# Attention products with the values stationary, and the router's transposes ahead of its logits

## The chip, the cores and the metric

The kernel runs on one core of a Trainium2 chip. The metric is the device time of one execution in microseconds. The kernel before took 1974.58 us, the median of three runs (1971.63 to 1975.39). TensorE (PE) is granted one of two clocks, 1.2 or 2.4 GHz; the profile prints the granted clock of a stretch as a share of the higher one.

## The reference

A decoder trunk of two layers over 256 tokens of 1024 channels in float32. Each layer has a token mixer and a feed-forward part, dense in layer 0 and routed to 2 of 8 experts in layer 1.

```
def _masked_softmax(s, mask):
    s = jnp.where(mask, s, NEG_INF)
    return jnp.where(mask, jax.nn.softmax(s, axis=-1), 0.0)
def token_mixing(h, ...):
    (nq, ..., mg) = split(h @ w_in)
    o_nsa = sum over (cmp, sel, win) of g_branch * softmax(q k) @ v   # 8 heads in 2 groups
    o_ret = silu(g) * normalised(retention(q, k, v))
    o_fox = softmax(q k * scale + decay) @ v                          # 8 heads, each with its own v
    merged = gates0*(o_nsa @ w_read_nsa) + gates1*(o_ret @ w_read_ret) + gates2*(o_fox @ w_read_fox)
    return merged @ w_out
def moe_ffn(h, ...):
    top_v, top_i = top_k(h @ w_router, 2)
    return sum over experts of gate * swiglu(h, w1[e], w3[e], w2[e])
```

## The kernel before

Weights come in chunks of 1 MB. ScalarE (ACT) copies a half of a chunk to `w_hi`, VectorE (DVE) makes the rest `w_lo`, and PE multiplies three pairs for each product (`mm3`, L746 to L748). The splits run `AHEAD` = 3 halves in front of PE.

In the token mixer the attention is spread over the projection. The string `SLOTS` (L189) is an order by hand: each slot names steps of the attention, then a quarter of a projection block (12 `mm3` steps, some 2.8 us of PE). The calls are `CALLS`, nine of them: 0 cmp, 1 sel, 2 win (head group 0), 3 cmp, 4 sel, 5 win (group 1), 6 retention, 7 and 8 fox. In a slot, `a1:5` turns the queries of call 5, `a2` and `a3` are its scores on PE and their mask and row maximum on DVE, `e0` and `e1` the exponentials on ACT for the first and the second 128 tokens, `b1` and `b2` PE's transposes of these probabilities from `S` by way of PSUM (`pT`) into `PT`, `b3` the product with the values (for cmp it goes with `b2`), `o` the transposes of a finished mixer's output and `s`, `d` pieces of the adaLN columns. Every engine walks the same string; DVE ends a slot with the piece's copies (`ended`) and the next split (`split_to`).

The product with the values (`attention_values`, L966 to L997) holds 128 x 128 probabilities stationary and moves 64 columns of values, so the result has tokens on partitions. DVE's `values` (L2134) then takes the reciprocal of the row sums, multiplies by the branch's gate, scales the result out of PSUM and adds it up in `o_sb`. At `o` PE turns `o_sb` in eight transposes, and ACT and DVE split the turned rows.

The router of layer 1 stands between the mixer and the experts: the normalised rows `y` are turned (`rows_T`), DVE scales them into `hf`, PE multiplies them with the router's weights `routw` (`logits`), a piece of the adaLN product follows (`ada_pair`, tiles `raw,csilu`), then the counts of the chosen (`rs,tab`), the gather of rows per expert (`sel,y`), and the experts' products.

Of the kernel before, what the change touches and what calls it, by code (L numbers as in the profile page):

```python
# [31 lines left out]
P = 128  # L32
# [312 lines left out]
P_COUNT = {"cmp": 1, "sel": 2, "win": 2, "ret": 0, "fox": 2}  # L345
S_SIGNALS = sum(S_COUNT[k] for k, _ in CALLS)
# [3 lines left out]
def build(nc, a, table, out):  # L350
    ctx = ExitStack()
    with ctx:
# [179 lines left out]
        p_ready = sem("p_ready")  # L532
        var_ready = sem("var_ready")
# [191 lines left out]
        def _(pe):  # L725
# [222 lines left out]
            def probabilities(sub, c, l):  # L948
# [4 lines left out]
                if kind == "cmp":  # L953
                    pe.wait_ge(p_ready, p_at + 1)
                    for t in range(TT):
                        turned([s[:, (t * HG + h) * 16:(t * HG + h) * 16 + NCMP] for h in range(HG)], P)
                elif sub == "b1":
                    pe.wait_ge(p_ready, p_at + 1)
                    turned([s[:, h * P:(h + 1) * P] for h in range(HG)], P)
                else:  # L960
                    pe.wait_ge(p_ready, p_at + 2)
# [4 lines left out]
            def attention_values(sub, c, l):  # L966
# [13 lines left out]
                dst = take_O()  # L980
                if kind == "cmp":
                    for t in range(TT):
                        for h in range(HG):
                            at = t * HG * HD + h * HD
                            ins = mm(dst[:, at:at + HD], PT[0:NCMP, (t * HG + h) * P:(t * HG + h + 1) * P], vc[0:NCMP, g, :])
                    ins.then_inc(O_full, 1)
                    return
                v0 = {"sel": C_NVS + g * HD, "win": C_NVW + g * HD, "fox": C_FV + g * HG * HD}[kind]
                vs = HD if kind == "fox" else 0
                for h in range(HG):  # L990
                    mm(dst[:, h * HD:(h + 1) * HD], PT[:, h * P:(h + 1) * P], proj[:, 0, v0 + h * vs:v0 + h * vs + HD])
                for h in range(HG):
                    for m in range(2):
                        at = (HG + h * 2 + m) * P
                        ins = mm(dst[:, (HG + h) * HD:(HG + h + 1) * HD], PT[:, at:at + P],
                                 proj[:, m, v0 + h * vs:v0 + h * vs + HD], m == 0, m == 1)
# [82 lines left out]
            for l in range(DEPTH):  # L1079
# [12 lines left out]
                for subs, kind, which, i in MIXES[l]:  # L1092
                    for sub, c in subs:
# [19 lines left out]
                        elif sub == "o":  # L1113
# [117 lines left out]
                else:  # L1231

                    dst = take_A()
# [8 lines left out]

                    logits(0)
                    rows_T(2, 3)
                    logits(1)
                    rows_T(3, 4)
# [11 lines left out]
                    ada_sum_early()  # L1258
                    pe.wait_ge(slots_ready, 1)
# [163 lines left out]
        def _(act):  # L1423
# [208 lines left out]
            for l in range(DEPTH):  # L1632
# [32 lines left out]
                for subs, kind, which, i in MIXES[l]:  # L1665
# [3 lines left out]
                    for sub, c in subs:  # L1669
# [17 lines left out]
                        elif sub in ("b1", "b2") and (t_uses(sub, c) or CALLS[c][0] == "ret"):  # L1687
                            evacuate_p(sub, c)
                        elif sub == "o":
# [141 lines left out]
        def _(dve):  # L1831
# [302 lines left out]
            def values(sub, c, l):  # L2134
# [24 lines left out]
                p_at = P_SIGNALS * l + sum(P_COUNT[k] for k, _ in CALLS[:c])  # L2159
                if kind == "cmp":  # L2160
                    if c == 0:
                        dve.wait_ge(sig_ready, 2 * l + 1)
                    dve.wait_ge(p_ready, p_at + 1)
                    sv = s[:, 0:P].rearrange("p (r n) -> p r n", n=16)[:, :, 0:NCMP]
                    link(V.tensor_reduce(st[:, 16:24], sv, AX_X, ALU.add))
                else:
                    dve.wait_ge(p_ready, p_at + 2)
                link(V.reciprocal(st[:, 24:32], st[:, 16:24]))
                coef = st[:, 24:32]
                if kind != "fox":  # L2170
                    coef = st[:, 32:40]
                    branch = {"cmp": 0, "sel": 1, "win": 2}[kind]
                    cv = coef.rearrange("p (t h) -> p t h", t=TT)
                    link(V.tensor_tensor(cv, st[:, 24:32].rearrange("p (t h) -> p t h", t=TT),
                                         gates3[:, :, branch * 8 + g * HG:branch * 8 + (g + 1) * HG], ALU.mult))
                    if kind == "cmp":
                        link(V.tensor_tensor(cv, cv, bc(cvalid.unsqueeze(2), [P, TT, HG]), ALU.mult))
                po, free = O_in()
                width = HG * HD
                src = po[:, :].rearrange("p (t h d) -> p t h d", t=TT, h=HG)  # L2180
                dst = o_sb[:, :, g * width:(g + 1) * width].rearrange("p t (h d) -> p t h d", h=HG)
                cf = coef.rearrange("p (t h) -> p t h", t=TT)
# [429 lines left out]
```

## Time and profile before

| what | value |
|---|---|
| median of three runs | 1974.58 us |
| the profiled execution | 1973.35 us, span 1971.6 us |
| mean granted clock | 0.985 |
| PE, DVE, ACT busy | 96%, 74%, 58% of the span |
| token mixers | about 50 to 355 us and 592 to 905 us |
| dense part | about 355 to 584 us |
| router, experts | 905 to 952 us, 952 to 1950 us |

In a timeline row the first number is the start in microseconds from the start of the span, the second the length, then engine, line, operation, output tile, input tiles, shapes and the number of instructions in the group; a bracket holds the idle time ahead of it and what ended it. A float32 product of the program shows as two instructions, a transpose as one. In a row of windows stand the window, its length, the busy time of each engine with its number of instructions, the granted clock, the share of the DMA engines and GB/s. In a row of grouped lines the last fields are busy us, mean ns of one, and idle before.

### The profile page before, as it was taken

The page shows a single profiled execution, that of the slowest core. Times are in us where ns is not written, and L with a number is a line of the kernel's source. Part 1 is how long each engine was busy: PE and PEld are TensorE (multiplying, and loading weights), DVE is VectorE, ACT ScalarE, POOL GpSimd, SP SyncE. Part 2 cuts the span into 40 slices and gives each one's busy share as a digit, 9 for nine tenths or more (in the row PEclk, how much of TensorE's full clock was granted, in tenths as well). Part 3 has the DMA queues.
Part 4 walks back from the last instruction along what each step waited for, and adds up shares of the span by engine and source line. Part 5 has one row for each costly group of instructions (what it writes and reads, how often), then busy time and mean ns, then how long its engine had stood idle before and what let it go on. Part 6 is the DMA issues. An engine that isn't in the chain of part 4 may idle for free.

```text
span 1971.6 us, 29864 instructions
## 1 busy us (share of the span) xinstructions
PE 1897.5 (96%) x10960; PEld 1472.4 (75%) x10960; DVE 1459.5 (74%) x1507; ACT 1141.8 (58%) x1245; POOL 92.4 (5%) x134
## 2 busy tenths in 40 slices
PE   5999999999999999998999999999999999999996
PEld 3878888789987888887776676766766767667774
DVE  3755565745567655657788888889888888888988
ACT  1544554334435545542567767777677676767773
POOL 0510100000004201000000000000000000000000
PEclk9999999999999999998899999999999999999998
DMA  8846435595557644353799999999999999999993
GB/s 316 290 155 233 152 128 171 198 332 183 185 192 232 221 150 150 128 171 129 278 371 343 354 343 358 353 343 355 343 362 354 342 346 349 355 348 345 358 365 135
DMA packets 275638, 533.10 MB, mean 270 GB/s; under 512 B 10768, under 2 KB 23392, under 8 KB 275424
## 3 DMA queue, kind: packets, MB, share of 16 engines
q1 hardware_dynamic: 275552, 531.91, 76.5%
q8 instruction: 60, 0.98, 0.2%
q14 instruction: 26, 0.21, 0.0%
HBM read 530.83 MB, written 1.05 MB: 270 GB/s over the span
## 4 chain that ended last, share of the span: by engine, by line
PE 86%; DVE 7%; ACT 3%; DVEq 2%; issue 1%; DMA 1%; SPq 0%; ACTq 0%
PE pA L746 17%; PE pA L747 17%; PE pA L748 17%; PE pA L751 8%; PE pO L751 7%; PE pO L746 5%; PE pO L747 5%; PE pO L748 5%; PE pT L804 3%; DVE w_lo L1851 1%; DVEq L2486 1%; DVE wide_lo L1896 1%; ACT w_hi L1434 1%; ACT wide_hi L1434 1%; DMA raw<-in_ffn_w 1%
## 5 line engine op out<-in xcount | busy, mean ns | idle before, releaser
L1896 DVE TENSOR_TENSOR wide_lo<-raw,wide_hi 128x2048 fp32r<-128x2048 f32 x336 | 761.6, 2290 | 120.6 <-ACT wide_hi L1434 101.6
L1434 ACT ACTIVATE wide_hi<-raw 128x2048 fp32r<-128x2048 f32 x336 | 644.3, 1920 | 212.0 <-PE pO L748 118.1
L1434 ACT ACTIVATE w_hi<-raw 128x1024 fp32r<-128x1024 f32 (+1 forms) x242 | 251.2, 1045 | 334.8 <-PE pA L748 235.8
L1851 DVE TENSOR_TENSOR w_lo<-raw,w_hi 128x1024 fp32r<-128x1024 f32 (+1 forms) x242 | 294.3, 1230 | 167.0 <-ACT w_hi L1434 157.9
L746 PE MATMUL pA<-wide_hi,x_lo 128*96 128x512 f32 x896 | 356.4, 398 | 1.6 <-DVE wide_lo L1896 1.0
L747 PE MATMUL pA<-wide_lo,x_hi 128*96 128x512 f32 x896 | 353.7, 395 | 0.0
L748 PE MATMUL pA<-wide_hi,x_hi 128*96 128x512 f32 x896 | 351.0, 392 | 0.0
L746 PE MATMUL pA<-w_hi,h_lo 128*128 128x512 f32 (+2 forms) x560 | 226.1, 404 | 14.7 <-DVE w_lo L1851 10.8
L748 PE MATMUL pA<-w_hi,h_hi 128*128 128x512 f32 (+2 forms) x560 | 216.8, 387 | 0.0
L747 PE MATMUL pA<-w_lo,h_hi 128*128 128x512 f32 (+2 forms) x560 | 216.7, 387 | 0.0
L746 PEld LDWEIGHTS pA<-wide_hi,x_lo 128*96 128x96 f32 x896 | 144.6, 161 | 65.3 <-issue 3.5
L748 PEld LDWEIGHTS pA<-wide_hi,x_hi 128*96 128x96 f32 x896 | 144.7, 162 | 63.0
L747 PEld LDWEIGHTS pA<-wide_lo,x_hi 128*96 128x96 f32 x896 | 144.4, 161 | 57.0
L746 PE MATMUL pO<-wide_hi,aT_lo 128*96 128x512 f32 x448 | 178.8, 399 | 1.1 <-DVE aT_lo L2454 1.1
L747 PE MATMUL pO<-wide_lo,aT_hi 128*96 128x512 f32 x448 | 176.5, 394 | 0.0
L748 PE MATMUL pO<-wide_hi,aT_hi 128*96 128x512 f32 x448 | 175.7, 392 | 0.0
L746 PEld LDWEIGHTS pA<-w_hi,h_lo 128*128 128x128 f32 x560 | 106.7, 191 | 41.9 <-issue 17.5
L748 PEld LDWEIGHTS pA<-w_hi,h_hi 128*128 128x128 f32 x560 | 106.7, 191 | 22.9
L747 PEld LDWEIGHTS pA<-w_lo,h_hi 128*128 128x128 f32 x560 | 107.1, 191 | 19.1
L751 PE MATMUL pA<-h_hi,w_lo 128*128 128x256 f32 x352 | 99.0, 281 | 0.8 <-DVE w_lo L1851 0.6
L751 PE MATMUL pA<-h_hi,w_hi 128*128 128x256 f32 x352 | 98.3, 279 | 0.0
L751 PE MATMUL pA<-h_lo,w_hi 128*128 128x256 f32 x352 | 98.3, 279 | 0.0
(273 smaller groups left out, 2272.7 us busy)
## 6 DMA issues: line engine op xcount, KB each, us to landing
raw<-in_moe_w SPq DMA_DIRECT2D x336, 1024.0 KB, 7.2
raw<-in_w_in SPq DMA_DIRECT2D x56, 1024.0 KB, 6.4
raw<-in_ada_w SPq DMA_DIRECT2D x48, 1024.0 KB, 6.8
raw<-in_ffn_w SPq DMA_DIRECT2D x33, 1024.0 KB, 5.2
raw<-in_w_out SPq DMA_DIRECT2D x8, 1024.0 KB, 5.1
raw<-in_cmp_k_w SPq DMA_DIRECT2D x4, 1024.0 KB, 7.7
raw<-in_cmp_v_w SPq DMA_DIRECT2D x4, 1024.0 KB, 11.1
raw<-in_w_read_nsa SPq DMA_DIRECT2D x4, 1024.0 KB, 6.1
```

The source lines that it names most:

```text
L746: nc.tensor.matmul(dst, xl, wh, start=first, stop=False, skip_group_check=True)
L747: nc.tensor.matmul(dst, xh, wl, start=False, stop=False, skip_group_check=True)
L748: return nc.tensor.matmul(dst, xh, wh, start=False, stop=last, skip_group_check=True)
L751: return nc.tensor.matmul(dst, lhsT, rhs, start=first, stop=last, skip_group_check=True)
L804: ins = nc.tensor.transpose(pt[0:m, i * width:i * width + n], src, ident[0:n, 0:n])
L1434: return nc.scalar.activation(dst, src, ACT.Copy)
L1851: V.tensor_tensor(w_lo[m][:, 0:n], raw[s][:, i * n:(i + 1) * n], w_hi[m][:, 0:n].bitcast(F32), ALU.subtract).then_inc(raw_done, 1)
L1896: V.tensor_tensor(wide_lo[m][:, :], raw[g][:, :], wide_hi[m][:, :].bitcast(F32), ALU.subtract).then_inc(raw_done, 2)
L2486: dve.drain().then_inc(gather_free, 1)
```

## The change

Values become stationary: in `attention_values` PE loads 64 columns of values and moves the turned probabilities, the even heads to output partitions 0 to 63 and the odd ones to 64 to 127. The result comes out turned, so at `o` of calls 0 and 2 (the sparse attention and fox) PE transposes nothing; ACT and DVE split `o_sb` directly. Scaling by the reciprocal sum and the gate can no longer follow the product, since tokens are then on the free axis: the new `scaled(t, c, l)` on DVE multiplies the probabilities in `S` in place, half by half, and signals `p_scaled`, for which PE's `b1` and `b2` now wait instead of `p_ready`. DVE's `values` is left with one copy or one addition. The list `LATE` holds calls 4 and 5, whose `b1` and `e1` share a slot. At the router `rows_T` of the next quarter precedes `logits`, and `keep_clock` multiplies zeros 8 times before the logits and 10 times after `ada_sum_early`.

```diff
@@ -343,6 +343,7 @@
+LATE = [c for subs, *_ in SLOTS for sub, c in subs if sub == "b1" and ("e1", c) in subs]
@@ -951,14 +953,14 @@
                 if kind == "cmp":
-                    pe.wait_ge(p_ready, p_at + 1)
+                    pe.wait_ge(p_scaled, p_at + 1)
                     for t in range(TT):
...
                 elif sub == "b1":
-                    pe.wait_ge(p_ready, p_at + 1)
+                    pe.wait_ge(p_scaled, p_at + 1)
                     turned([s[:, h * P:(h + 1) * P] for h in range(HG)], P)
                 else:
-                    pe.wait_ge(p_ready, p_at + 2)
+                    pe.wait_ge(p_scaled, p_at + 2)
                     for p0 in range(0, HG, 2):
@@ -978,22 +980,30 @@
+                rows_of = lambda odd: dst[odd * HD:(odd + 1) * HD, :]
...
-                    for t in range(TT):
-                        for h in range(HG):
-                            at = t * HG * HD + h * HD
-                            ins = mm(dst[:, at:at + HD], PT[0:NCMP, (t * HG + h) * P:(t * HG + h + 1) * P], vc[0:NCMP, g, :])
+                    late = PT[0:NCMP, 0:2 * HG * P].rearrange("p (t j o n) -> p t j o n", t=TT, j=2, o=2)
+                    for odd in range(2):
+                        ins = mm(rows_of(odd).rearrange("p (t j n) -> p t j n", t=TT, j=2), vc[0:NCMP, g, :], late[:, :, :, odd, :])
...
-                vs = HD if kind == "fox" else 0
-                for h in range(HG):
-                    mm(dst[:, h * HD:(h + 1) * HD], PT[:, h * P:(h + 1) * P], proj[:, 0, v0 + h * vs:v0 + h * vs + HD])
-                for h in range(HG):
-                    for m in range(2):
-                        at = (HG + h * 2 + m) * P
-                        ins = mm(dst[:, (HG + h) * HD:(HG + h + 1) * HD], PT[:, at:at + P],
-                                 proj[:, m, v0 + h * vs:v0 + h * vs + HD], m == 0, m == 1)
+                first = PT[:, 0:HG * P].rearrange("p (j o n) -> p j o n", j=2, o=2)
+                second = PT[:, HG * P:3 * HG * P].rearrange("p (j o m n) -> p j o m n", j=2, o=2, m=2)
+                steps = [(0, 0, True, True), (1, 0, True, False), (1, 1, False, True)]
+                if kind == "fox":
+                    for j in range(2):
+                        for t, m, opens, closes in steps:
+                            for odd in range(2):
+                                c0 = v0 + (2 * j + odd) * HD
+                                p_t = first[:, j, odd, :] if t == 0 else second[:, j, odd, m, :]
+                                ins = mm(rows_of(odd)[:, (2 * t + j) * P:(2 * t + j + 1) * P], proj[:, m, c0:c0 + HD], p_t, opens, closes)
+                else:
+                    for t, m, opens, closes in steps:
+                        for odd in range(2):
+                            p_t = first[:, :, odd, :] if t == 0 else second[:, :, odd, m, :]
+                            ins = mm(rows_of(odd)[:, t * SEQ:(t + 1) * SEQ].rearrange("p (j n) -> p j n", j=2),
+                                     proj[:, m, v0:v0 + HD], p_t, opens, closes)
@@ -1110,7 +1120,7 @@
-                        elif sub == "o":
+                        elif (sub, c) == ("o", 1):
@@ -1230,6 +1240,16 @@
+                    spare = pA[b.A.slot(b.A.n + 3)]
+                    evacuated(b.A, A_free, 4)
+                    def keep_clock(n):
+                        for _ in range(n):
+                            mm(spare[:, :].rearrange("p (k n) -> p k n", k=CK), zeros[:, :],
+                               zeros[:, :].unsqueeze(1).broadcast_to([P, CK, P]))
+                    keep_clock(8)
@@ -1240,10 +1260,10 @@
+                    rows_T(2, 3)
...
-                    rows_T(2, 3)
+                    rows_T(3, 4)
...
-                    rows_T(3, 4)
@@ -1256,6 +1276,7 @@
                     ada_sum_early()
+                    keep_clock(10)
                     pe.wait_ge(slots_ready, 1)
@@ -1686,6 +1707,11 @@
+                        elif sub == "o" and c != 1:
+                            act.wait_ge(o_ready, 3 * l + c + 1)
+                            for q in range(2):
+                                copy(oT_hi[c][:, 2 * q:2 * q + 2, :].rearrange("p j (t n) -> p t j n", t=TT),
+                                     o_sb[:, q, :].rearrange("p (t j n) -> p t j n", t=TT, j=2)).then_inc(oT_hi_ready, 1)
@@ -2156,40 +2182,40 @@
                     return
-                p_at = P_SIGNALS * l + sum(P_COUNT[k] for k, _ in CALLS[:c])
+                po, free = O_in()
+                dst = o_sb[:, g, :]
+                if kind in ("cmp", "fox"):
+                    V.tensor_copy(dst, po[:, :]).then_inc(free, 1)
+                else:
+                    V.tensor_tensor(dst, dst, po[:, :], ALU.add).then_inc(free, 1)
+                freed(b.O, O_free)
+                if c in WHOLE:
+                    dve.drain().then_inc(o_ready, 1)
+            def scaled(t, c, l):
+                kind, g = CALLS[c]
+                st = stat[:, (c % 2) * 40:(c % 2) * 40 + 40]
+                s = S[c % 2]
+                dve.wait_ge(p_ready, P_SIGNALS * l + sum(P_COUNT[k] for k, _ in CALLS[:c]) + t + 1)
                 if kind == "cmp":
...
                         dve.wait_ge(sig_ready, 2 * l + 1)
-                    dve.wait_ge(p_ready, p_at + 1)
                     sv = s[:, 0:P].rearrange("p (r n) -> p r n", n=16)[:, :, 0:NCMP]
                     link(V.tensor_reduce(st[:, 16:24], sv, AX_X, ALU.add))
+                    t0, nt, width = 0, TT, NCMP
                 else:
-                    dve.wait_ge(p_ready, p_at + 2)
-                link(V.reciprocal(st[:, 24:32], st[:, 16:24]))
-                coef = st[:, 24:32]
+                    t0, nt, width = t, 1, (t + 1) * P
+                    sv = s[:, HG * P * t:HG * P * t + HG * width].rearrange("p (h n) -> p h n", h=HG)
+                at = slice(24 + t0 * HG, 24 + (t0 + nt) * HG)
+                link(V.reciprocal(st[:, at], st[:, 16 + t0 * HG:16 + (t0 + nt) * HG]))
                 if kind != "fox":
-                    coef = st[:, 32:40]
                     branch = {"cmp": 0, "sel": 1, "win": 2}[kind]
-                    cv = coef.rearrange("p (t h) -> p t h", t=TT)
-                    link(V.tensor_tensor(cv, st[:, 24:32].rearrange("p (t h) -> p t h", t=TT),
-                                         gates3[:, :, branch * 8 + g * HG:branch * 8 + (g + 1) * HG], ALU.mult))
+                    cv = st[:, at].rearrange("p (t h) -> p t h", t=nt)
+                    link(V.tensor_tensor(cv, cv, gates3[:, t0:t0 + nt, branch * 8 + g * HG:branch * 8 + (g + 1) * HG], ALU.mult))
                     if kind == "cmp":
                         link(V.tensor_tensor(cv, cv, bc(cvalid.unsqueeze(2), [P, TT, HG]), ALU.mult))
-                po, free = O_in()
-                width = HG * HD
-                src = po[:, :].rearrange("p (t h d) -> p t h d", t=TT, h=HG)
-                dst = o_sb[:, :, g * width:(g + 1) * width].rearrange("p t (h d) -> p t h d", h=HG)
-                cf = coef.rearrange("p (t h) -> p t h", t=TT)
-                for t in range(TT):
-                    to = dst[:, t] if kind in ("cmp", "fox") else o_part[:, t * width:(t + 1) * width].rearrange("p (h d) -> p h d", h=HG)
-                    ins = V.tensor_tensor(to, src[:, t], bc(cf[:, t].unsqueeze(2), [P, HG, HD]), ALU.mult)
-                ins.then_inc(free, 1)
-                freed(b.O, O_free)
-                if kind in ("sel", "win"):
-                    both = o_sb[:, :, g * width:(g + 1) * width]
-                    link(V.tensor_tensor(both, both, o_part[:, :].rearrange("p (t n) -> p t n", t=TT), ALU.add))
-                if c in WHOLE:
-                    dve.drain().then_inc(o_ready, 1)
+                V.tensor_tensor(sv, sv, bc(st[:, at].unsqueeze(2), [P, nt * HG, width]), ALU.mult).then_inc(p_scaled, 1)
@@ -2246,6 +2272,9 @@
+                        if sub == "b2" and c in LATE:
+                            scaled(1, c, l)
+                    for sub, c in subs:
@@ -2256,6 +2285,12 @@
+                        elif sub == "o" and c != 1:
+                            for q in range(2):
+                                dve.wait_ge(oT_hi_ready, 6 * l + 2 * c + q + 1)
+                                turns = lambda to: to[c][:, 2 * q:2 * q + 2, :].rearrange("p j (t n) -> p t j n", t=TT)
+                                V.tensor_tensor(turns(oT_lo), o_sb[:, q, :].rearrange("p (t j n) -> p t j n", t=TT, j=2),
+                                                turns(oT_hi).bitcast(F32), ALU.subtract).then_inc(oT_ready, 1)
@@ -2270,6 +2305,11 @@
+                    for sub, c in subs:
+                        if sub == "e0" and CALLS[c][0] == "cmp" or sub == "e1":
+                            scaled(0, c, l)
+                        elif sub == "b1" and CALLS[c][0] in ("sel", "win", "fox") and ("e1", c) not in subs:
+                            scaled(1, c, l)
```

DVE around call 5 (`win`, group 1), from the mask of its last scores (`S_108<-pO,tab`) over the projection's copies to the next splits, before:

```order
L2059 TENSOR_TENSOR S_108<-pO,tab 128x512 [waits O_full]
L2065 TENSOR_REDUCE stat<-S_108 128x4 [waits O_free0]
L2066 TENSOR_SCALAR stat<-stat 128x4 [waits dve_link]
L2168 RECIPROCAL stat<-stat 128x8 [waits p_ready]
L2174 TENSOR_TENSOR stat<-stat,gates_80 128x8 [waits dve_link]
L2185 TENSOR_TENSOR tmp<-pO,stat 128x256 [waits O_full,dve_link]
L2185 TENSOR_TENSOR tmp<-pO,stat 128x256
L2190 TENSOR_TENSOR o_sb<-o_sb,tmp 128x2x256 [waits O_free1]
L1866 TENSOR_TENSOR mod<-pT,cols 128x4 [waits T_full,dve_link]
L2201 COPY proj<-pA 128x512 [waits half_used] x2
L1851 TENSOR_TENSOR w_lo_62<-raw_54,w_hi_58 128x1024 [waits hi_ready]
```

and the same place on DVE now:

```order
L2085 TENSOR_TENSOR S_108<-pO,tab 128x512 [waits O_full]
L2091 TENSOR_REDUCE stat<-S_108 128x4 [waits O_free0]
L2092 TENSOR_SCALAR stat<-stat 128x4 [waits dve_link]
L2190 TENSOR_TENSOR o_sb<-o_sb,pO 128x512 [waits O_full]
L1892 TENSOR_TENSOR mod<-pT,cols 128x4 [waits T_full,O_free1]
L2227 COPY proj<-pA 128x512 [waits half_used] x2
L1877 TENSOR_TENSOR w_lo_62<-raw_54,w_hi_58 128x1024 [waits hi_ready]
L2211 RECIPROCAL stat<-stat 128x4 [waits p_ready]
L2215 TENSOR_TENSOR stat<-stat,gates_80 128x4 [waits dve_link]
L2218 TENSOR_TENSOR S_108<-S_108,stat 128x512 [waits dve_link]
```

The values' five instructions of call 4 shrank to one addition, and behind the copies and a split stands the scaling of call 5's first half, which `b1:5` on PE waits for.

PE at the router, from the adaLN sum (`tab,acc`) over the turned rows (`tab,y`) to the logits (`routw,hf`), before:

```order
L870 MATMUL pO<-tab,acc 128x128 [waits O_free1,O_free0]
L751 MATMUL pA<-routw,hf 128x8 [waits hf_ready,A_free2]
L751 MATMUL pA<-routw,hf 128x8 x3
L804 MATMUL pT<-tab,y 128x128 [waits T_free0,y_ready]
L804 MATMUL pT<-tab,y 128x128 x3
L751 MATMUL pA<-routw,hf 128x8 [waits hf_ready]
L751 MATMUL pA<-routw,hf 128x8 x3
L804 MATMUL pT<-tab,y 128x128 [waits T_free1]
L804 MATMUL pT<-tab,y 128x128 x3
```

and PE at the router now:

```order
L872 MATMUL pO<-tab,acc 128x128 [waits O_free1,O_free0]
L753 MATMUL pA<-zeros 128x512 [waits A_free0,A_free1,A_free3,A_free2]
L753 MATMUL pA<-zeros 128x512 x7
L806 MATMUL pT<-tab,y 128x128 [waits T_free0,y_ready,A_free2]
L806 MATMUL pT<-tab,y 128x128 x3
L753 MATMUL pA<-routw,hf 128x8 [waits hf_ready]
L753 MATMUL pA<-routw,hf 128x8 x3
L806 MATMUL pT<-tab,y 128x128 [waits T_free1]
L806 MATMUL pT<-tab,y 128x128 x3
```

Eight products of zeros stand ahead, and each group of transposes moved one group of logits forward.

## Rows read from the trace of the kernel before

**Rows 1.** Windows: us, busy of PE, PEld, DVE, ACT, POOL, clock, DMA, GB/s

```profile
137.00:205.00 68.00, 68.00 (x601) 56.11 (x600) 37.42 (x64) 31.53 (x80) 1.87 (x1) 1.00 0.57 201
...
952.00:1950.00 998.00, 995.57 (x4560) 704.06 (x4559) 874.00 (x633) 708.63 (x547) 0.00 (x0) 1.00 0.96 345
```

**Rows 2.** Timeline of PE, call 1's value product and its neighbours

```profile
137.68 1.13 PE L751 MATMUL pO<-kT,qT 64*128 64x256 f32 x4
...
142.47 2.79 PE L751 MATMUL pO<-proj,PT 128*128 128x64 f32 x24
145.19 0.64 PE L751 MATMUL pO<-raw,csilu 128*32 128x128 f32 x16
```

**Rows 3.** Timeline of PE, call 3's value product to call 4's first transposes

```profile
177.41 1.99 PE L751 MATMUL pO<-vc,PT 15*128 15x64 f32 x16
179.33 0.50 PE L746 MATMUL pA<-w_hi,h_lo 128*128 128x512 f32 x1
...
182.44 0.60 PE L804 MATMUL pT<-tab,S 128*128 128x128 f32 x4
```

**Rows 4.** Timeline of PE, the output's transposes of the sparse attention

```profile
228.37 1.04 PE L804 MATMUL pT<-tab,o_sb 128*128 128x128 f32 x8
229.16 0.48 PE L746 MATMUL pA<-w_hi,h_lo 128*128 128x512 f32 x1
```

**Rows 5.** Timeline of PE, router

```profile
918.35 1.95 PE L751 MATMUL pO<-raw,csilu 128*32 128x128 f32 x64
...
925.09 1.71 PE L751 MATMUL pA<-routw,hf 128*128 128x8 f32 x8 [2.21 <-DVE hf L1999]
...
936.91 2.30 PE L751 MATMUL pA<-rs,tab 128*128 128x8 f32 x10
...
942.57 6.93 PE L751 MATMUL pA<-sel,y 128*128 128x96 f32 x32 [3.05 <-DVE mod L1866]
...
951.61 0.47 PE L746 MATMUL pA<-wide_hi,x_lo 128*96 128x512 f32 x1 [0.29 <-DVE x_lo L2439]
```

**Rows 6.** Lines of DVE by shape, 100 to 300 us

```profile
L1851 DVE TENSOR_TENSOR w_lo<-raw,w_hi 128x1024 fp32r<-128x1024 f32 x41 | 51.0, 1249 | 17.9 <-ACT w_hi L1434 15.5
...
L2185 DVE TENSOR_TENSOR tmp<-pO,stat 128x256 f32<-128x256 f32 x8 | 3.0, 419 | 12.9 <-PE pO L751 12.9
L2190 DVE TENSOR_TENSOR o_sb<-o_sb,tmp 128x512 f32<-128x512 f32 x4 | 2.8, 693 | 0.1
...
L2168 DVE RECIPROCAL stat<-stat 128x8 f32<-128x8 f32 x8 | 1.6, 197 | 0.1
```

**Rows 7.** Timeline of DVE around calls 4 and 5

```profile
181.31 1.23 DVE L1851 TENSOR_TENSOR w_lo<-raw,w_hi 128x1024 fp32r<-128x1024 f32 x1
...
195.51 1.22 DVE L2065 TENSOR_REDUCE stat<-S 128x4 f32<-128x1024 f32 x1
...
199.27 1.28 DVE L2201 COPY proj<-pA 128x512 f32<-128x512 f32 x2
```

**Rows 8.** Timeline of PE, call 5's first transposes

```profile
200.31 0.60 PE L804 MATMUL pT<-tab,S 128*128 128x128 f32 x4
```

**Rows 9.** Windows around idle stretches and at the router, columns as in rows 1

```profile
110.00:112.00 2.00, 0.48 (x4) 0.37 (x4) 0.00 (x0) 1.99 (x4) 0.00 (x0) 1.00 0.96 371
113.00:119.00 6.00, 6.00 (x15) 4.26 (x14) 3.27 (x6) 1.13 (x2) 0.00 (x0) 0.50 0.01 3
661.00:669.00 8.00, 6.48 (x35) 5.08 (x34) 3.71 (x8) 5.31 (x7) 0.00 (x0) 1.00 0.26 100
926.00:949.00 23.00, 19.95 (x141) 19.03 (x142) 12.39 (x39) 2.30 (x4) 0.00 (x0) 0.50 0.48 173
```

**Rows 10.** Timeline of DVE, router

```profile
925.16 0.99 DVE L1999 TENSOR_SCALAR hf<-pT,mod 128x256 f32<-128x256 f32 x2
...
931.44 2.29 DVE L1896 TENSOR_TENSOR wide_lo<-raw,wide_hi 128x2048 fp32r<-128x2048 f32 x1 [0.21 <-issue]
```

**Rows 11.** Timeline of PE, products of zeros within the experts

```profile
974.37 0.61 PE L751 MATMUL pO<-zeros 128*128 128x512 bf16 x2
```

More of the change, by code:

```diff
@@ L532, in build @@
         p_ready = sem("p_ready")
+        p_scaled = sem("p_scaled")
         var_ready = sem("var_ready")
```

## The prediction

> **What bounds the kernel now.** I read the windows by stage first: the reader is to see which engine is full in each. In the token mixer's middle PE is busy for all of 68 us and DVE for 37.42, at granted clock 1.00; in the experts PE is busy 995.57 of 998 us [rows 1]. So in both PE's own work sets the time, and DVE costs only where PE is made to wait for it. The experts follow the router with no slack, so what the router gains reaches the end in full. Then the timelines of PE for the price of each changed piece, those of DVE for what a new wait would meet, and the windows around idle stretches for the clock. In the router PE runs at 0.50 from 926 to 949 us [rows 9]: every product there costs double.
>
> The sum is made against the profiled execution, 1973.35 us; the median of the runs shown is 1.2 us above it.
>
> **Values stationary (removes PE time).** A product with the values of sel, win and fox is 24 instructions and takes 145.19 - 142.47 = 2.72 us, 0.113 each [rows 2]. Now it is 12 instructions for sel and win with 256 columns moved, or 24 for fox with 128 columns, and two of them, for the even and the odd heads, write different halves of the output partitions. The trace has no pair of 64-column products. The nearest row is the adaLN piece with 32 columns: 64 float32 instructions of 128 columns in 1.95 us [rows 5], so 0.12 us for every four, where the value product shows 0.113 us for one of only 64 columns: the four run side by side. I take two abreast for 64 columns, at 0.12 us a pair of 128 columns: fox 12 x 0.12 = 1.46, sel and win 6 x 0.24 = 1.46. For cmp, 1.92 us before [rows 3], there are 4 instructions of 512 columns, 2 x 0.49 = 0.98. Changing between full and split columns costs a little; in rows 2 the adaLN piece starts 0.07 us before the modelled end of the value product, so I take 0.1 a call. A call of sel, win or fox gains 2.72 - 1.56 = 1.16 us, a cmp 1.92 - 1.08 = 0.84 us. With 12 and 4 such calls in two layers: 13.9 + 3.4 = 17.3 us. The other end: nothing side by side. A group of four 256-column float32 instructions takes 1.13 us, 0.28 each [rows 2], which makes 12 x 0.28 = 3.4 us and a loss of 0.7 a call.
>
> The Trainium skill, "TensorEngine Tiling (Array Packing)", Theoretical Speedup, gives up to 2x for 64 columns; the row of four abreast agrees. The same page speaks against the change in Key Properties: changing the tiling mode drains the engine. If a drain cost a whole 256-column instruction of 0.28 us at the entry and at the exit (an estimate from rows 2), 16 calls would pay 9 us instead of my 1.6 and the forecast would be 1970; the early start of the adaLN piece in rows 2 speaks against that.
>
> **No transposes at `o`.** Eight transposes take 229.16 - 228.37 = 0.79 us [rows 4]; two such steps in each layer go: 3.2 us. ACT and DVE do there what they did, from another source. PE gains 17.3 + 3.2 = 20.5 us.
>
> **Scaling ahead of the transposes (adds DVE time and waits).** DVE's prices: 1.25 us for 1024 columns, 0.69 for 512, 0.42 for 256, 0.20 for a small one [rows 6]. A call of sel or win loses two small ones, two of 256 and one of 512 (1.93) and gains four small ones, 512 and 1024 scaled and one of 512 added (3.4): +1.5 us; fox +2.0, cmp about +0.1. A layer: 4 x 1.5 + 2 x 2.0 + 0.2 = 10 us. On the average that lies in DVE's idle 30 of 68 us [rows 1]. But `b1` and `b2` on PE now wait for it, and all of PE's later products queue behind them. At two places there is no slack, since `b1` and `e1` share a slot and the scaling stands behind a split.
>
> Call 4: the split that ended at 181.31 + 1.23 = 182.54 [rows 7] comes 1.0 earlier, as the four small ones and two of 256 of call 3 make way for one of 512 (1.64 - 0.69); the scaling of 512 with two small ones is 1.1, so it is done at 182.7. PE arrives at 182.44 - 0.84 = 181.6 [rows 3]. Wait 1.1 us.
>
> Call 5: DVE's row maximum ends at 195.51 + 1.22 = 196.73; then one small one, the addition of 0.69, one small one, the copies of 1.28 [rows 7], a split of 1.25 and the scaling of 1.1: 201.5. PE arrives at 200.31 - 1.16 = 199.15 [rows 8]. Wait 2.4 us.
>
> For the other scaled halves I find slack of 0.3 to 0.7 us in the slots, and allow 1 us a layer, an estimate. Waits: 4.5 a layer, 9 us in all; between 4 (half of it, if the slots behind take some up) and 20 (all of DVE's added time).
>
> **The clock in the mixers.** At 110.1 us PE idles 1.5 us, and from 113 to 119 us the clock is 0.50; the same wait near 661 us leaves it at 1.00 [rows 9]. Six us at half clock do three us of work: 3 us lost. I charge the two waits at call 5 with 2.5 us each, 5 in all; ends 0 and 12 (four waits at 3).
>
> **The router.** At full clock, the transposes moved ahead let DVE make its four pairs of `hf` one behind the other from 925.16 on at 0.99 each [rows 10]: done at 928.2, the split of 2.29 at 930.5 instead of 933.7, 3.2 earlier. The counts would halve (2.30 to 1.15) and the gather too (6.93 to 3.47) [rows 5]: 3.2 + 1.15 + 3.47 = 7.8, or some 8 with the end of the piece that delays the counts now. The zeros: 0.61 us for two with the tail of the second [rows 11], some 0.23 each, so 8 take 1.8 us in an idle time of 2.21 and 10 take 2.3 in one of 3.05 [rows 5]: nothing at full clock; without that cover 4.1 us. But a new gap opens: PE ends the adaLN piece near 930.6 (1.95 at full clock) and the counts wait for DVE until 933.4, 2.8 us without zeros. By the idle of 1.5 us above I expect half clock after it, over counts and zeros: counts from 933.4 to 935.7, a short piece of adaLN and zeros of 4.5 us to 940.7, and the gather at full clock again to 944.1, where it ended at 942.57 + 6.93 = 949.5 [rows 5]: 5.4 us. I take 5.5; ends 8 and a loss of 1 (half clock all through, zeros of 4.5 us in the 3.05).
>
> **Sum.** -20.5 + 9 + 5 - 5.5 = -12: 1961.4 us for the profiled execution, 1962.6 for the median. I predict 1963 us.
>
> **Rivals.** (a) The router stays at half clock; the zeros don't help. For it: it fell after the idle of 2.21 us [rows 5], and the zeros leave some 0.4 of that. Against: 1.8 of it is filled. -20.5 + 9 + 5 + 1 = -5.5: 1969. (b) The 64-column products don't run side by side, since the row that I read is of another width. Sel and win lose 0.7 each (8 x 0.7 = 5.6), fox with 24 at 0.12 loses 0.2 (0.8), cmp 4 x 0.5 = 2.0 loses 0.1 (0.4), `o` gains 3.2; PE arrives later, so about 1 us of wait a layer remains (2), with one fall of the clock (2.5). 5.6 + 0.8 + 0.4 - 3.2 + 2 + 2.5 - 5.5 = +2.6: 1977, no change by 0.2%. (c) Slower: DVE becomes the pace-maker of the attention slots. Its splits stand behind the scaling in the same queue, PE waits at each `b1` and `b2`, and each of the four long waits drops the clock: -20.5 + 20 + 12 - 5.5 = +6: 1981. It decides from the point where over 14 of the 20 us that DVE gains come out on PE's path. For it: the scaling is in the path of every call; against it, DVE's idle 45% in rows 1. (d) The waits are half as long, no clock is lost, the router holds: -20.5 + 4.5 - 8 = -24: 1951.
>
> **Chances.** Forecast 0.45 (its own range 1956 to 1967), (a) 0.22, (b) 0.12, (c) 0.09, (d) 0.12. What a measurement of this kernel can tell from no change is about 0.2%, 4 us: 1970.6 to 1978.5. Faster takes the forecast, (d) and most of (a): 0.77; the same takes (b) and the rest of (a): 0.14; slower is (c): 0.09. Leaving out (c) and the outer parts of (b) and (d), the range is 1950 to 1974.
>
> **What would show it.** In the profile after, the value products of sel and win should take 1.4 to 1.6 us between their start and the next group's (3.2 to 3.4 would be rival b); PE should wait for DVE's scaling at `b1` of call 4 (1.1) and call 5 (2.4) in both layers, with a clock of 0.50 behind the second; the gap after the adaLN piece in the router should be 2 to 3 us, and the first expert's product come near 939.6 us instead of 951.61 [rows 5], all of the sum. The prediction is wrong if PE's waits in a mixer exceed 8 us, if the router's clock stays 0.50 up to the experts, or if the experts' stretch changes length at all, since nothing in it changed.

## The result and the profile after

The changed kernel took 1962.9 us, the median of five runs (1960.09 to 1963.92); the ratio to the kernel before is 0.994, with a 95% interval of 0.9928 to 0.9951. The prediction was 1963. The profiled execution took 1960.09 us, its span is 1958.3 us.

The timeline of PE after, at call 1 (which answers to [rows 2]), at the first transposes of calls 4 and 5 ([rows 3, 8]) and in the router ([rows 5]); the columns are those of the rows before:

```profile
140.76 1.51 PE L753 MATMUL pO<-PT,proj 128*64 128x256 f32 x12
142.21 1.95 PE L753 MATMUL pO<-raw,csilu 128*32 128x128 f32 x64
...
178.54 0.66 PE L806 MATMUL pT<-tab,S 128*128 128x128 f32 x4 [0.88 <-DVE S L2218]
...
197.50 0.66 PE L806 MATMUL pT<-tab,S 128*128 128x128 f32 x4 [2.10 <-DVE S L2218]
...
912.65 1.95 PE L753 MATMUL pO<-raw,csilu 128*32 128x128 f32 x64
915.98 1.09 PE L806 MATMUL pT<-tab,y 128*128 128x128 f32 x8 [1.38 <-DVE y L2015]
...
917.02 1.89 PE L753 MATMUL pA<-zeros 128*128 128x512 bf16 x8
...
923.86 3.60 PE L753 MATMUL pO<-raw,csilu 128*32 128x128 f32 x64
927.52 1.28 PE L753 MATMUL pA<-rs,tab 128*128 128x8 f32 x10
...
928.80 2.32 PE L753 MATMUL pA<-zeros 128*128 128x512 bf16 x10
932.12 3.81 PE L753 MATMUL pA<-sel,y 128*128 128x96 f32 x32 [1.00 <-DVE mod L1892]
...
938.03 0.48 PE L748 MATMUL pA<-wide_hi,x_lo 128*96 128x512 f32 x1 [0.29 <-DVE x_lo L2479]
```

The reader is to see: twelve products in 142.21 - 140.76 = 1.45 us where 24 took 2.72; two waits for DVE's scaling (`S`, L2218) that were not there; and a router whose counts and gather run at full speed (1.28 and 3.81 us, where [rows 5] has 2.30 and 6.93) while the adaLN piece ahead of them takes 3.60 where it took 1.95. What PE waits for in the layers, as engine and line waited for, us in total, times and longest, for the mixer of layer 0:

```profile
PE pT L806 <- DVE S L2218: 3.3, 3, 2.1
PE pO L753 <- ACT kT L1455: 1.5, 1, 1.5
```

Only the first line is new; layer 1 shows the same 3.3 us, and 0.9 more at the forget gates (`DVE fox`). The windows of the changed kernel behind the idle time ahead of call 1, behind the wait of call 5 in layer 0 and around it in layer 1, and in the router, columns as in [rows 1]:

```profile
113.00:119.00 6.00, 6.00 (x18) 4.30 (x17) 3.74 (x10) 0.27 (x2) 0.00 (x0) 0.56 0.01 3
199.00:203.00 4.00, 4.00 (x54) 3.18 (x45) 0.00 (x0) 1.92 (x9) 0.00 (x0) 1.00 0.68 213
738.00:740.00 2.00, 0.40 (x2) 0.40 (x3) 1.93 (x5) 0.67 (x1) 0.00 (x0) 0.89 0.00 0
740.00:743.00 3.00, 3.00 (x52) 2.51 (x54) 0.69 (x1) 2.24 (x8) 0.00 (x0) 0.51 0.02 5
924.00:927.00 3.00, 3.00 (x60) 2.77 (x62) 2.78 (x10) 0.22 (x1) 0.00 (x0) 0.50 0.02 5
928.00:937.00 9.00, 8.00 (x62) 6.56 (x62) 6.60 (x25) 1.81 (x2) 0.00 (x0) 1.00 0.88 309
```

PE's group starts, aligned piece by piece with those of before, give the steps in layer 0: a call of sel, win or fox is 1.17 us shorter (1.28 of the product less 0.10 ahead of it for sel), a cmp 0.92, each `o` 0.87; the wait of call 4 takes back 1.04, that of call 5 2.27, `b2:5` 0.45. From the keys of call 1 to the end of the mixer that is 6.1 us less in layer 0. In layer 1 of the two profiled executions the same steps gave nothing on balance: half-clock stretches in the mixer (592 to 905 us) cost PE 4.9 us after and nothing before (busy time weighted with what the clock lacked of 1.00, in windows of 2 us). From the router's adaLN piece to the first expert's product it is 25.4 us after and 33.3 before. The profiles' split into mixers and router thus hangs on where the clock happened to be low, and the runs have to decide it.

One stretch that the change does not touch grew: the dense part, from PE's wait for `h_lo` behind the mixer of layer 0 to its wait of 3.0 us for `y` ahead of layer 1's, took 232.1 us before and 233.4 after. Behind a wait of 2.1 us for DVE's `mod`, which both kernels have, the clock fell in the second profile alone (the kernel before, then the changed one):

```profile
426.00:434.00 8.00, 4.83 (x28) 4.05 (x29) 4.49 (x9) 1.74 (x3) 0.00 (x0) 1.00 1.05 389
420.00:428.00 8.00, 5.53 (x26) 4.88 (x27) 3.54 (x6) 1.53 (x2) 0.00 (x0) 0.79 1.05 393
```

### The profile page after: what moved, and what is told of

Read it like the earlier page. It is cut to its first block, busy times and chain, and to the rows that moved or that the text cites. A ratio compares the mean times of both kernels' runs of the same rounds, so it can differ in the third digit from the quotient of the medians.

```text
span 1958.3 us, 29535 instructions
## 1 busy us (share of the span) xinstructions
PE 1880.5 (96%) x10802; PEld 1438.2 (73%) x10802; DVE 1478.7 (76%) x1531; ACT 1143.9 (58%) x1245; POOL 95.6 (5%) x134
## 4 chain that ended last, share of the span: by engine, by line
PE 83%; DVE 9%; ACT 3%; DMA 2%; DVEq 2%; issue 1%; SPq 1%; ACTq 0%
PE pA L748 17%; PE pA L749 16%; PE pA L750 16%; PE pA L753 8%; PE pO L748 5%; PE pO L749 5%; PE pO L750 5%; PE pO L753 5%; PE pT L806 3%; DVE w_lo L1877 2%; DVE wide_lo L1922 1%; DMA tab<-in_tables 1%; DVEq L2526 1%; ACT w_hi L1455 1%; ACT wide_hi L1455 1%
```

## The experiments

All were timed in five rounds beside the kernel before, whose medians in the three groups were 1974.22, 1974.08 and 1973.56 us.

**The parts alone.** The value products, the `o` and the scaling with the old router:

```
-                    spare = ...; evacuated(b.A, A_free, 4); def keep_clock(n): ...
-                    keep_clock(8)
-                    rows_T(2, 3); logits(0); rows_T(3, 4); logits(1)
+                    logits(0); rows_T(2, 3); logits(1); rows_T(3, 4)
-                    keep_clock(10)
```

> The new value products, the output without transposes and the scaling ahead, with the router as before. My theory, by which the router's stretch lost 33.26 - 25.38 = 7.9 us and the rest of the gain is the mixers': 1962.9 + 7.9 = 1971 us, 4 us below before, with PE waits for DVE's scaling of about 0.9 and 2.1 us at calls 4 and 5. Rival (the whole gain is the router's, the mixers give back in waits and clock what PE saves): 1974 to 1975 us.

Measured: 1966.17 us, ratio 0.9964 (0.9952 to 0.9976). And the reverse, the new router on the kernel before:

```
+                    spare = ...; evacuated(b.A, A_free, 4); def keep_clock(n): ...
+                    keep_clock(8)
-                    logits(0); rows_T(2, 3); logits(1); rows_T(3, 4)
+                    rows_T(2, 3); logits(0); rows_T(3, 4); logits(1)
+                    keep_clock(10)
```

> The kernel before with the router's new order and the zeros alone. My theory: 1974.6 - 7.9 = 1966.7 us, the first expert's product about 8 us earlier. Rival (the router's clock was held only by chance in the profiled execution, the mixers carry the gain): 1970 us or more. Rival (all of the gain is the router's): 1963 us.

Measured: 1969.86 us, ratio 0.9976 (0.9967 to 0.9985). Both of my numbers missed, and in the same sense: by the medians the mixers give 8.0 us (4.7 to 9.5 by the interval) and the router 4.4 (3.0 to 6.5). Together 12.4, the change's own 11.7 within the noise, so as far as the intervals tell the parts add. The 7.9 us read from one pair of profiles was too much for the router: over all the profiles of this section, the stretch from the router's adaLN piece to the first expert's product takes 25.4 to 27.7 us with both groups of zeros (seven profiles) and 31.1 to 33.3 without any (three), and the pair that I compared first lies nearly at the two ends. In the profile of the router alone, half clock lay over the counts and most of the second zeros, and the gather ran at full clock:

```profile
934.03 2.30 PE L751 MATMUL pA<-rs,tab 128*128 128x8 f32 x10
...
936.44 3.61 PE L751 MATMUL pA<-zeros 128*128 128x512 bf16 x10
939.88 3.74 PE L751 MATMUL pA<-sel,y 128*128 128x96 f32 x32
```

The same profiles show where the mixers' gain is steady. From PE's wait for `win_lo` to its wait for `h_lo`, layer 0's mixer takes 268.6 us in all six profiles with the changed mixers as they are, and 274.8 in both with the old ones. Layer 1's takes 262.9 to 267.3 against 267.5. The dense part behind layer 0 takes 233.4 to 234.9 against 232.1, each time with half clock behind its wait of 2 us; why the clock fell there with the changed mixers and not with the old ones isn't shown.

**The overlap.** The even heads' products first, then the odd ones':

```
-                    for t, m, opens, closes in steps:
-                        for odd in range(2):
+                    for odd in range(2):
+                        for t, m, opens, closes in steps:
```

> The changed kernel, with the products of sel, win and fox in another order: all of the even heads' (partitions 0 to 63), then all of the odd heads' (64 to 127), so that two neighbours share their 64 columns and cannot run side by side. The same number of instructions and columns. My theory (two abreast): sel and win go from 1.45 to about 3.0 us, fox from 1.46 to 2.9; 8 x 1.6 + 4 x 1.4 = 18 us, of which 3 are taken from the waits at call 5: 1977 to 1980 us. Rival (the gain comes from fewer weight loads, not from running side by side): 1963 us.

Measured: 1967.82 us, ratio 0.9971 (0.996 to 0.9982): 4.9 us above the changed kernel, neither number. The trace shows why. The order undoes the overlap only in part: the starts of the twelve instructions fall into two rows of six, each mostly 0.216 us apart, one from 142.94 and one from 143.43 on. That the second row is the odd half's is read from this spacing; it began when three of the even half's six had yet to start, and not behind the sixth. So a second experiment took the second half of the columns away:

```
-                rows_of = lambda odd: dst[odd * HD:(odd + 1) * HD, :]
+                rows_of = lambda odd: dst[0:HD, :]
```

> The changed kernel with all products with the values written to output partitions 0 to 63, the odd heads over the even ones (it leaves the odd heads' result out), so that no two can run side by side, in whatever order they are taken. My theory (in the kernel with one half first the second half's products still started after two of the first's, so that experiment undid the overlap only in part): 12 products at 0.216 each are 2.6 us for sel and win, 24 at 0.109 are 2.6 for fox, 4 at 0.43 are 1.8 for cmp, so every call loses 1.1 us or 0.8: 12 x 1.1 + 4 x 0.8 = 16 us, less some 4 of the waits for DVE: 1974 to 1976 us, what the kernel before takes; without the overlap the values stationary gain nothing. Rival (the overlap is worth only the 5 us of that experiment): 1968 us.

The whole time, 3004.79 us, says nothing: with the odd heads' results missing the router chooses other rows, as it seems, and the experts take 2050 us instead of 1020. Its mixers can be read. The same product in the timeline of PE with one half first:

```profile
142.94 2.00 PE L753 MATMUL pO<-PT,proj 128*64 128x256 f32 x12
144.87 0.41 PE L753 MATMUL pO<-raw,csilu 128*32 128x128 f32 x5
```

and with all in one half:

```profile
143.78 2.80 PE L753 MATMUL pO<-PT,proj 128*64 128x256 f32 x12
146.52 0.32 PE L753 MATMUL pO<-raw,csilu 128*32 128x128 f32 x4
```

From start to the next group's start: 1.45 us alternating, 1.93 one half first, 2.74 in one half, and 2.72 before (for fox 1.46, 2.38, 2.76 and 2.62). Aligned with the changed kernel, every sel, win and fox call loses 1.29 to 1.30 us and every cmp 0.85. Making the values stationary gains nothing in itself; all of the product's gain is two halves of the columns at work at once. Without it the mixer of layer 0 takes 278.1 us, 3.4 more than before the change, although the transposes at `o` are gone; a fall of the clock near 254 us, which the profile before lacks, is at most 1.7 of that.

**The waits.** DVE scales the first half of calls 4 and 5 one slot earlier, ahead of the copies and the split:

```
-                        if sub == "e0" and CALLS[c][0] == "cmp" or sub == "e1":
+                        if sub == "e0" and (CALLS[c][0] == "cmp" or c in LATE) or sub == "e1" and c not in LATE:
                             scaled(0, c, l)
```

> The changed kernel, with DVE's scaling of the first half for calls 4 and 5 moved one slot forward, behind the first exponentials and ahead of the projection's copies and the split. My theory: the waits of 0.88 and 2.10 us go in both layers, 6 us, and the fall of the clock behind the second of them in layer 1 (1.6 us in the profile) too: 1955 to 1957 us. Rival (DVE sets the pace, the split is late instead and PE waits for weights): 1961 to 1963 us.

Measured: 1954.66 us, ratio 0.9899 (0.9884 to 0.9913), 8.2 us below the changed kernel and just under my numbers. DVE at call 5, from the addition of call 4's values to the split:

```profile
192.73 0.68 DVE L2190 TENSOR_TENSOR o_sb<-o_sb,pO 128x512 f32<-128x512 f32 x1
...
193.92 0.69 DVE L2218 TENSOR_TENSOR S<-S,stat 128x512 f32<-128x512 f32 x1
194.53 1.28 DVE L2227 COPY proj<-pA 128x512 f32<-128x512 f32 x2
195.95 2.36 DVE L1877 TENSOR_TENSOR w_lo<-raw,w_hi 128x1024 fp32r<-128x1024 f32 x2
```

and what PE waits for in the mixer of layer 0:

```profile
PE pO L753 <- ACT kT L1455: 1.5, 1, 1.5
...
PE pA L748 <- DVE w_lo L1877: 0.5, 1, 0.5
PE pT L806 <- DVE S L2218: 0.3, 1, 0.3
```

The waits of 0.88 and 2.10 us are gone, and the split that stood ahead of the scaling costs no more than before (`w_lo` 0.5). DVE had the time; the scaling stood in the wrong place of its queue. 6 of the 8.2 us are these waits. In the two profiles layer 0's mixer is 3.4 us shorter and layer 1's 7.6, with one half-clock stretch of 3.4 us in place of three; that the rest of the 8.2 is the clock is argued, not shown.

**The router's parts.** Without both groups of zeros:

```
-                    keep_clock(8)
-                    keep_clock(10)
```

> The changed kernel without the two groups of zero products; the transposes still stand ahead of the logits. My theory (order and zeros share the router's gain of some 4 us: the order lets DVE's scaled rows follow each other, the zeros keep the clock up for counts and gather): the router at 0.50 for most of its length, the gather 6 to 7 us instead of 3.8: 1965 to 1966 us. Rival (the order alone does it): 1963 us.

Measured: 1967.97 us, ratio 0.9964 (0.9952 to 0.9976), above both numbers. With the zeros and the old order:

```
-                    rows_T(2, 3); logits(0); rows_T(3, 4); logits(1)
+                    logits(0); rows_T(2, 3); logits(1); rows_T(3, 4)
```

> The changed kernel with the zero products but with the logits of a quarter ahead of the next transposes, as before. My theory: DVE's scaled rows wait for PE between the quarters again, 1 to 2 us more: 1964 to 1965 us. Rival (the order carries the router's gain, the zeros do nothing): 1966 us. Rival (the zeros carry all of it): 1963 us.

Measured: 1961.76 us, ratio 0.9934 (0.9921 to 0.9948), below all three numbers and nearest to the rival that gives the zeros all. So the zeros carry all of the router's gain that can be measured (1967.97 against 1962.9 us is 5.1) and the order none: with the zeros 1961.76 us in the old order and 1962.9 in the new one, without them 1966.17 (the mixers alone) and 1967.97, both at a ratio of 0.9964. DVE's scaled rows and its copy of the logits in the changed kernel, and then, with the start of PE's adaLN piece, in the kernel with the old order:

```profile
919.47 3.26 DVE L2025 TENSOR_SCALAR hf<-pT,mod 128x256 f32<-128x256 f32 x6
...
925.29 0.17 DVE L2422 COPY rs<-pA 128x16 f32<-128x16 f32 x1
```

```profile
915.81 1.95 PE L753 MATMUL pO<-raw,csilu 128*32 128x128 f32 x64
...
924.11 0.99 DVE L2025 TENSOR_SCALAR hf<-pT,mod 128x256 f32<-128x256 f32 x2 [0.50 <-PE pT L806]
925.40 0.99 DVE L2025 TENSOR_SCALAR hf<-pT,mod 128x256 f32<-128x256 f32 x2 [0.29 <-PE pT L806]
...
928.95 0.17 DVE L2422 COPY rs<-pA 128x16 f32<-128x16 f32 x1
```

In the new order the rows follow each other without a pause; in the old one the pauses, at full clock, come to 0.8 us. The router without zeros, timeline of PE and one window:

```profile
919.65 1.09 PE L806 MATMUL pT<-tab,y 128*128 128x128 f32 x4 [2.25 <-DVEq L2017]
...
931.62 2.30 PE L753 MATMUL pA<-rs,tab 128*128 128x8 f32 x10
...
937.25 6.79 PE L753 MATMUL pA<-sel,y 128*128 128x96 f32 x32 [3.02 <-DVE mod L1881]
```

```profile
918.00:942.00 24.00, 19.33 (x137) 18.43 (x138) 14.55 (x44) 3.85 (x5) 0.28 (x1) 0.53 0.50 179
```

The clock is 0.53 over the 24 us, counts and gather cost double, as before the change. Then each group alone:

```
-                    keep_clock(10)
```

> The changed kernel with the eight zero products ahead of the logits and without the ten behind the counts. My theory (each group shortens the stretch at half clock that the router's idle times start): the clock is back for the counts as in the changed kernel, but PE idles 3.4 us ahead of the gather and part of the gather runs at half clock, 2 to 3 us more: 1965 to 1966 us. Rival (the first group alone is enough, since the gather has begun before the clock falls): 1963 us.

Measured: 1964.37 us, ratio 0.9956 (0.9943 to 0.997), between my numbers and the rival's; by the medians 3.6 us less than without zeros and 1.5 more than with both. And the other:

```
-                    keep_clock(8)
```

> The changed kernel with the ten zero products behind the counts and without the eight ahead of the logits. My theory: half clock from the second idle time on, over logits, adaLN piece and counts, some 2 us of which DVE's work hides; the zeros, at half clock, bring the clock back before the gather: 1964 to 1966 us. Rival (the second group is what counts, since the gather is the longest piece): 1963 us. Rival (the zeros at half clock outlast the idle time and delay the gather): 1967 us or more.

Measured: 1964.84 us, ratio 0.9959 (0.9945 to 0.9972), within my numbers. The router with the first group alone, and then with the second alone:

```profile
927.26 2.30 PE L753 MATMUL pA<-rs,tab 128*128 128x8 f32 x10
...
932.88 6.76 PE L753 MATMUL pA<-sel,y 128*128 128x96 f32 x32 [3.02 <-DVE mod L1891]
```

```profile
931.79 2.30 PE L753 MATMUL pA<-rs,tab 128*128 128x8 f32 x10
...
934.19 4.47 PE L753 MATMUL pA<-zeros 128*128 128x512 bf16 x10
938.46 4.40 PE L753 MATMUL pA<-sel,y 128*128 128x96 f32 x32
```

The traces show what each does: with the first alone the gather falls into half clock (6.76 us), with the second alone logits, adaLN piece and counts do, but the zeros, though at half clock, bring the clock back for most of the gather (4.40). What each group is worth by itself the times don't tell: the intervals of either overlap with that of both groups and with that of none. In the profiles the stretch from the adaLN piece to the first expert's product is 30.0 us with the first group alone and 31.9 with the second alone; the latter is within what it takes without any (31.1 to 33.3).

**The idle time ahead of call 1.** On top of the early scaling, six products of zeros into the bank that the scores of call 1 then overwrite:

```
+                if sub == "a2" and c == 1:
+                    early_O = take_O()
+                    for _ in range(6):
+                        mm(early_O[:, :]..., zeros[:, :], zeros[:, :]...)
                 if sub == "a2":
                     copied(("a", c))
```

> The kernel with the early scaling and, in both layers, six products of zeros in front of the wait of 1.5 us for the keys of call 1, into the bank that the scores then overwrite. My theory (the idle time of 1.5 us lets the clock fall there, always in layer 0 so far and in some executions in layer 1): no 0.50 behind 110 and 657 us, 3.3 + 1.7 us less: 1949 to 1951 us. Rival (the zeros don't count as work for the clock, or it falls at the next wait instead): 1954 to 1955 us.

Measured: 1949.74 us, ratio 0.9875 (0.986 to 0.989), by the medians 4.9 us less than with the early scaling alone, whose interval it just overlaps, and 24.3 us below the kernel before. The window that was at 0.56 in the changed kernel, and PE's zeros:

```profile
109.47 1.47 PE L753 MATMUL pO<-zeros 128*128 128x512 bf16 x6
111.14 1.04 PE L753 MATMUL pO<-kT,qT 64*128 64x128 f32 x7 [0.21 <-ACT kT L1461]
```

```profile
113.00:119.00 6.00, 5.08 (x24) 3.68 (x24) 4.05 (x13) 1.71 (x3) 0.00 (x0) 1.00 0.01 3
```

The idle time shrank from 1.5 to 0.2 us and the clock held there. A shorter fall came later, near 120 us, behind a wait of 0.9 us for the forget gates that the slow stretch had hidden:

```profile
117.00:123.00 6.00, 5.91 (x25) 4.60 (x26) 3.50 (x7) 3.03 (x11) 0.00 (x0) 0.72 0.00 0
```

So the zeros gained little where they stand. The mixer of layer 0 with the early scaling alone, and then with the zeros, by PE's first and last wait:

```profile
80.88 0.38 PE L748 MATMUL pA<-w_hi,win_lo 128*128 128x256 f32 x1 [1.15 <-DVE win_lo L2118]
346.08 0.47 PE L748 MATMUL pA<-w_hi,h_lo 128*128 128x512 f32 x1 [1.17 <-DVE h_lo L2043]
```

```profile
80.45 0.38 PE L748 MATMUL pA<-w_hi,win_lo 128*128 128x256 f32 x1 [1.14 <-DVE win_lo L2124]
345.34 0.47 PE L748 MATMUL pA<-w_hi,h_lo 128*128 128x512 f32 x1 [1.17 <-DVE h_lo L2049]
```

That is 265.2 and 264.9 us; layer 1's mixer takes 259.7 and 259.3. The rest of the 4.2 us between the two profiles lies outside the mixers, where the kernels are the same and the half-clock stretches were shorter in the second. My number came out, but what these zeros are worth is not shown.

## Why the prediction was right

**The products with the values** (13.9 + 3.4 us forecast): right in size and reason. 1.17 and 0.92 us a call were measured for 1.16 and 0.84, and the experiment in one half shows that all of it is the overlap, as the Trainium skill, "TensorEngine Tiling (Array Packing)", Theoretical Speedup, has it for 64 columns (2.74 to 1.45 us is 1.9x). The drain that the Trainium skill names on the same page, in Key Properties, costs little here: the block ahead of the product grew by 0.10 us, not by a whole product, so the trace keeps my price and not the 9 us. Where the pricing was off is rival (b): I gave a product of 256 columns that runs by itself 0.28 us, from the scores; by itself it takes 0.216 to 0.23, so without the overlap a call would lose nothing where I charged 0.7 us.

**No transposes at `o`** (3.2 us): 0.87 us each, 3.5 in all.

**The waits** (9 us): the two large ones at the places named, and for the reason named, since moving the scaling ahead of the split removed them. They measured 0.88, 2.10 and 0.29 where 1.1, 2.4 and 1.0 stood, 6.6 us in the two layers, and 0.9 at the forget gates of layer 1, which I had not named.

**The clock in the mixers** (5 us): half right. In layer 0 it stayed up behind the wait of call 5 (1.00 from 199 to 203 us), in layer 1 it fell to 0.50 for some 3.4 us, which cost at most 1.7. But layer 1's mixer had two more such falls, behind other waits, and lost 4.9 us by them all, and the sum put the dense part, 1.3 us longer here and up to 2.8 elsewhere, at nothing. The same idle times were followed by falls in some profiles and not in others, so one pair of profiles cannot price it; mixers alone gave 8.0 us where the sum has 6.5.

**The router** (5.5 us): the time is close to the 4.4 measured alone, but the step that failed is "the transposes moved ahead let DVE make its four pairs of `hf` one behind the other": I gave the order 3.2 us, and it is worth nothing that the runs can tell. With the zeros, PE at full clock serves DVE's rows almost as fast in the old order: from the adaLN piece's start to the copy of the logits 13.1 us with the old order and 12.6 with the new, and without zeros 15.4 before, 14.6 with the mixers alone and 15.4 with the new order. So of the 3.2 us the changed kernel's profile shows 2.8, but 2.3 of them come in the old order too: what looked like a matter of order was the clock, and the zeros, which I had down for the counts and the gather alone, are what moves it. The second half: I expected half clock over counts and zeros, behind a gap of 2.8 us. In the changed kernel's profile it came earlier, over the adaLN piece (924 to 927 us), which then filled that gap (1.7 us: the counts start 3.66 us after the piece, which takes 1.95 at full clock) and cost nothing. In the profile of the router alone it came where I had it: counts 2.30 us, ten zeros 3.61, the gather at full clock again with 3.74, and 27.3 us for the stretch against 33.3, close to the 5.5 of the sum. Where the clock falls in the router differs from profile to profile.

**The sum** came out at 1963 because the mixers were forecast 1.5 us too low and the router 1.1 too high by the medians, each less than its interval can tell. That these cancel to within 0.4 us, and that the falls of the clock in layer 1, two of them unplaced, come to the 5 us that I charged, is luck; the products, the transposes and the two waits are not. The first expert's product came at 938.03 us, where I had 939.6.

## What to carry to other kernels

When two small products write different column halves of the array, price them by the pair, and check the price with a kernel that puts both in one half: that, and not another order, takes the overlap away. When a change puts work in front of a consumer, look at what already stands in the producer's queue at that place; here one slot forward was worth 8 us with nothing else changed. Where a stretch runs at half clock behind idle times, test the filling of the idle time apart from a change of order: here the filling gave all that could be measured. Price the clock from runs and from several profiles, since its falls differ between executions, and look at the stretches that the change leaves alone as well.

## What the runs showed of the hardware

PE starts a product for the free half of the columns while earlier ones for the other half are still waiting: with six and then six, the second half's first product started 0.49 us after the first half's, with three of the first half's yet to start, and 0.81 of the 1.29 us of the overlap was kept (1.93 us between 1.45 and 2.74); with twelve and then twelve of half the length, 0.38 of 1.30 (fox, 2.38 us). In the profiles here, products of zeros in bfloat16 kept the granted clock at 1.00 where an idle time of 1.5 us else was followed by 0.50 in layer 0. Run at half clock ahead of the gather, they were followed by full clock in it (gather 4.40 us behind them, 6.79 without).
